# A two-layer block in float32r: the order of the first projection's column chunks

## The chip, the cores and the metric

The kernel runs on one core of a Trainium2 chip. The metric is the device time of one execution in microseconds (us). Engines: PE is TensorE (matrix products and transposes), ACT is ScalarE, DVE is VectorE, POOL is GpSimd, SP is SyncE, which here only issues transfers.

## What is computed

The reference has two layers on 256 tokens of 1024 channels. The change lies in the first layer's attention, whose first step is one wide projection `z = u @ w_in`, u being the normed input:

```
u = rms_norm(h, g_mix[i])
z = u @ w_in[i]
q_a, k_a, v_a, q_b, k_b, v_b, f_b, gate_logits = jnp.split(z, SPLIT_POINTS, axis=-1)
# widths:  512  128  128  512  512  512  8  2048
y_a = sliding_window_attention(q_a (8 heads), k_a, v_a (2 heads), sinks) @ w_br_swa[i]
# forgetting attention, per head:
log_f = log_sigmoid(f_b + b_forget);  c = cumsum(log_f)
s = q_b k_b^T * scale + c[query] - c[key], causal;  softmax;  times v_b
y_b = (that) @ w_br_fox[i]
mixed = gates[0] * y_a + gates[1] * y_b;  h = h + mixed @ w_mix_out[i]
```

A feed-forward part, an embedding gate, and a second layer follow. They are not touched.

## The kernel before, in words

**Products.** A float32 product is made of three passes. Both operands are split into an upper half (rounded to float32r) and a lower half (the rest), and PE computes upper x upper, upper x lower and lower x upper into the same PSUM bank (`mm3`, L1587 to L1589). So every piece of weight goes through a small pipeline: SP loads it into one of 8 slots of `raw`; ACT copies it into `w_hi` (one of 4 slots, L552); DVE subtracts and writes `w_lo` (L982); PE uses both. Counting semaphores tie the steps: `landed`, `hi_done`, `lo_done`, `units_used`. A piece is called a unit: two contraction tiles of 128 rows by up to 512 columns. Each unit takes 12 products (2 contraction tiles x 2 row tiles x 3). ACT and DVE run `AHEAD` = 3 units ahead of PE.

**Order.** Each engine has its own program, written out by hand, in order. `CH1` lists the column chunks of `w_in`, four units each. Before: chunk 0 has k_a, v_a and the 8 forget columns (264 columns), then q_a, q_b, k_b, v_b (512 each), then four chunks of gate logits, which PE works on in turn with the heads of the attention. Chunks use PSUM banks 0, 1 and 2, 3 alternately.

**Start.** SP issues the first half of x (two transfers), unit 0, the second half of x, then units 1 to 7, small vectors and the constant tables. ACT issues g_mix, the identity, and the forget columns of all four units of chunk 0 as one transfer (L617). PE runs 14 filler products of ones (`ones_products`), transposes g_mix and the first half of x (L1667), and runs 5 more fillers. ACT and DVE copy the transposed x, scaled, as upper and lower half (`wide_hi` L572, `wide_lo` L998), in turn with the splits of units 0 to 2.

**Eviction of the chunks.** ACT copies each chunk out of its banks, scaled by the norm's factor (`to_nat`, L612): queries and keys to `nat`, from where PE transposes them one chunk later (`natT_bank`) and DVE copies them to `qaT`, `ka_pad`, `qbT`, `kb_pad` (L1031, L1041, L1019); values go to `va_pad` and `vb_pad`; the forget columns go to `fz`.

**Forget gates.** DVE adds the bias; ACT computes ln(1 + exp(-|f|)) by Abs, Exp, Ln (L668, L670, L672); DVE forms the logs; PE sums them over the tokens by products with a triangle of ones (L1738 to L1740, `cum_done`); ACT and DVE copy the sums as upper and lower half (L675, L1127). `pick_tables` (L1094, L1096) makes on DVE a table of 0 and 1 for each of the 8 forgetting heads, with two casts each; a product of that table with the sums adds them to a head's scores. Before, all this runs inside chunks 1 to 4.

**Heads.** The loop over n = 0 to 19 has 16 heads, 8 of the sliding window, then 8 forgetting ones. In iteration n each engine does:

- PE: the 12 products of unit 20 + n, the scores of head n (L1773), the transposition of the probabilities of head n - 2 (`head_pt`, L1675), the output of head n - 3 (`head_pv`, L1686, L1687)
- ACT: the upper half of unit 23 + n, the copy of the transposed probabilities of head n - 2 (L605), the exponentials of head n (L595), which need DVE's row minima
- DVE: the lower half of unit 23 + n, scores and row minima of head n (L1051, `head_min`), the probabilities of head n - 1 (L1061, `head_norm`)

## Time and profile before

| | |
|---|---|
| median of 3 runs | 857.9 us (857.74 to 858.56) |
| profiled execution, its own time | 857.91 us |
| its span in the profile | 856.2 us |
| PE busy | 837.1 us, 98% of the span |
| DVE busy | 609.5 us, 71% |
| ACT busy | 464.6 us, 54% |
| POOL busy | 52.3 us, 6% |
| transfers | 170.45 MB, mean 199 GB/s |

The span runs from the first to the last instruction of the profiled execution; its own time contains a little more around it. Busy time of PE counts a product from its start to its modelled end, and products overlap, so the distance between two starts tells more than the duration of one. "Idle before" a group of instructions is given with what released the engine from its wait.

### The profile page before, as it was taken

To read this page: it belongs to the slowest core of one execution; us is meant where nothing else is said; L and a number is where in the kernel's file an instruction comes from. 1 tells how busy PE (TensorE), PEld (TensorE's weight loads), DVE (VectorE), ACT (ScalarE), POOL (GpSimd) and SP (SyncE) were. 2 spreads that over 40 slices of the span, in tenths; PEclk is the share of its full clock that TensorE was granted. 3 is DMA by queue.
4 is the path that set the end of the run, shared out by engine and by line. 5 is a ranking of instruction groups with operands and counts; after the bars stand their busy time and mean duration, and the time that the engine had idled before them with its cause. 6 is when DMAs were issued, how large, how long until landed. Compare 5 with 4: busy or idle time off the path is not lost.

```text
span 856.2 us, 12217 instructions
## 1 busy us (share of the span) xinstructions
PE 837.1 (98%) x4240; PEld 707.7 (83%) x4240; DVE 609.5 (71%) x947; ACT 464.6 (54%) x739; POOL 52.3 (6%) x68
## 2 busy tenths in 40 slices
PE   7999999999999999999999999999998999999996
PEld 7888888889888888877888888888887888888885
DVE  3666665867888888898767986565676766556656
ACT  4745665446555555677744446445444454445443
POOL 3000000102000000110200000011000000000000
PEclk9999999999999999999999999999999999999999
DMA  9764443597999999633664664545544465664641
GB/s 303 262 168 139 123 124 124 157 370 257 360 331 337 335 325 353 215 113 110 222 181 140 172 208 125 162 147 170 182 128 146 146 200 181 210 195 148 204 139 49
DMA packets 87560, 170.45 MB, mean 199 GB/s; under 512 B 7088, under 2 KB 33944, under 8 KB 87520
## 3 DMA queue, kind: packets, MB, share of 16 engines
q1 hardware_dynamic: 81040, 142.53, 51.9%
q0 software_dynamic: 5280, 27.30, 9.2%
q8 instruction: 23, 0.38, 0.2%
q10 hardware_dynamic: 1200, 0.10, 0.1%
q14 instruction: 17, 0.14, 0.0%
HBM read 168.84 MB, written 1.05 MB: 198 GB/s over the span
## 4 chain that ended last, share of the span: by engine, by line
PE 92%; DVE 3%; issue 1%; ACT 1%; DMA 1%; POOL 0%; ACTq 0%; DVEq 0%; POOLq 0%
PE B L1587 20%; PE B L1589 19%; PE B L1588 19%; PE B L1625 15%; PE B L1627 8%; PE B L1667 2%; PE B L1773 1%; PE B L1686 1%; PE B L1675 1%; DMA raw<-in_w_in_dram 1%; DVE w_lo L982 1%; PE B L1687 1%; PE B L1942 1%; PE B L1953 1%; DVE Z L1324 0%
## 5 line engine op out<-in xcount | busy, mean ns | idle before, releaser
L982 DVE TENSOR_TENSOR w_lo<-raw,w_hi 128x1024 fp32r<-128x1024 f32 (+3 forms) x156 | 187.1, 1210 | 80.8 <-ACT w_hi L552 79.0
L1587 PE MATMUL B<-w_hi,xT 128*128 128x512 f32 (+3 forms) x584 | 231.2, 396 | 3.8 <-DVE w_lo L982 3.1
L1589 PE MATMUL B<-w_hi,xT 128*128 128x512 f32 (+3 forms) x584 | 224.3, 384 | 0.0
L1588 PE MATMUL B<-w_lo,xT 128*128 128x512 f32 (+3 forms) x584 | 223.8, 383 | 0.0
L552 ACT ACTIVATE w_hi<-raw 128x1024 fp32r<-128x1024 f32 (+3 forms) x156 | 158.8, 1030 | 85.4 <-PE B L1589 80.6
L1587 PEld LDWEIGHTS B<-w_hi,xT 128*128 128x128 f32 x584 | 110.8, 190 | 24.5 <-issue 3.2
L1589 PEld LDWEIGHTS B<-w_hi,xT 128*128 128x128 f32 x584 | 110.5, 189 | 21.7
L1588 PEld LDWEIGHTS B<-w_lo,xT 128*128 128x128 f32 x584 | 110.9, 190 | 19.4
L1625 PE MATMUL B<-xT,w_hi 128*128 128x512 f32 x352 | 124.6, 398 | 1.8 <-DVE xT L1327 1.6
L1627 PE MATMUL B<-xT,w_lo 128*128 128x256 f32 x352 | 98.8, 281 | 0.0
L1552 DVE TENSOR_TENSOR w_lo<-raw,w_hi 128x1024 fp32r<-128x1024 f32 x60 | 71.7, 1221 | 29.0 <-ACT w_hi L949 29.0
L949 ACT ACTIVATE w_hi<-raw 128x1024 fp32r<-128x1024 f32 x60 | 62.0, 1054 | 41.2 <-PE B L1627 32.0
L1220 DVE TENSOR_TENSOR w_lo<-raw,w_hi 128x1024 fp32r<-128x1024 f32 x56 | 66.9, 1220 | 21.1 <-ACT w_hi L755 20.2
L1625 PEld LDWEIGHTS B<-xT,w_hi 128*128 128x128 f32 x352 | 66.1, 188 | 18.3 <-DVE xT L1327 1.8
L1587 PE MATMUL B<-w_hi,sT 128*128 128x512 f32 x200 | 79.3, 396 | 0.3 <-DVE w_lo L982 0.2
L1625 PE MATMUL B<-sT,w_hi 128*128 128x512 f32 x224 | 79.2, 397 | 0.0
L1589 PE MATMUL B<-w_hi,sT 128*128 128x512 f32 x200 | 78.1, 391 | 0.0
L1588 PE MATMUL B<-w_lo,sT 128*128 128x512 f32 x200 | 77.9, 390 | 0.0
L755 ACT ACTIVATE w_hi<-raw 128x1024 fp32r<-128x1024 f32 x56 | 57.6, 1053 | 35.2 <-PE B L1627 32.0
L1627 PEld LDWEIGHTS B<-xT,w_lo 128*128 128x128 f32 x352 | 66.5, 189 | 0.4
L1627 PE MATMUL B<-sT,w_lo 128*128 128x256 f32 x224 | 62.9, 281 | 0.0
L1228 DVE SCALAR_TENSOR_TENSOR Z<-Z,small 128x1536 f32<-128x1536 f32 x28 | 50.7, 1811 | 1.4 <-DMA Z<-in_w_ada_dram 1.4
(231 smaller groups left out, 993.3 us busy)
## 6 DMA issues: line engine op xcount, KB each, us to landing
raw<-in_w_in_dram SPq DMA_DIRECT2D x84, 512.0 KB, 3.7
raw<-in_w_ff_dram SPq DMA_DIRECT2D x64, 512.0 KB, 7.5
Z<-in_w_ada_dram POOLq DMA_DIRECT2D x32, 768.0 KB, 7.7
raw<-in_w_ffn_gate_dram SPq DMA_DIRECT2D x44, 256.0 KB, 3.6
raw<-in_w_ffn_up_dram SPq DMA_DIRECT2D x44, 256.0 KB, 4.4
raw<-in_w_ffn_down_dram SPq DMA_DIRECT2D x20, 512.0 KB, 4.4
raw<-in_w_mix_out_dram SPq DMA_DIRECT2D x8, 512.0 KB, 3.7
raw<-in_w_ple_gate_dram SPq DMA_DIRECT2D x8, 512.0 KB, 4.5
```

The costliest lines, as they stand in the source:

```text
L552: nc.scalar.activation(w_hi[:, u % SPLIT, :, 0:n], raw[:, st.slot[u], :, 0:n], ACT.Copy).then_inc(hi_done, 1)
L755: nc.scalar.activation(w_hi[:, u % SPLIT, :, :], raw[:, st.slot[u], :, :], ACT.Copy).then_inc(hi_done, 1)
L949: nc.scalar.activation(w_hi[:, u % SPLIT, :, :], raw[:, st.slot[u], :, :], ACT.Copy).then_inc(hi_done, 1)
L982: nc.vector.tensor_tensor(w_lo[:, u % SPLIT, :, 0:n], raw[:, st.slot[u], :, 0:n], w_hi[:, u % SPLIT, :, 0:n].bitcast(F32), ALU.subtract).t ...
L1220: nc.vector.tensor_tensor(w_lo[:, u % SPLIT, :, :], raw[:, st.slot[u], :, :], w_hi[:, u % SPLIT, :, :].bitcast(F32), ALU.subtract).then_in ...
L1228: nc.vector.scalar_tensor_tensor(ada_acc[:, 1536 * q:1536 * (q + 1)], ada_raw[:, q, :], silu_now, ada_acc[:, 1536 * q:1536 * (q + 1)], ALU ...
L1552: nc.vector.tensor_tensor(w_lo[:, u % SPLIT, :, :], raw[:, st.slot[u], :, :], w_hi[:, u % SPLIT, :, :].bitcast(F32), ALU.subtract).then_in ...
L1587: nc.tensor.matmul(bank, xh, wh, start=start, stop=False)
L1588: nc.tensor.matmul(bank, xh, wl, start=False, stop=False)
L1589: return nc.tensor.matmul(bank, xl, wh, start=False, stop=stop)
L1625: nc.tensor.matmul(B[:, i, :], w_hi[:, s, kk, cols], x2[:, kt0 + kk, :, :].rearrange("p e n -> p (e n)"), start=first and kk == 0, stop=False)
L1627: m = nc.tensor.matmul(B[:, i, SEQ:2 * SEQ], w_lo[:, s, kk, cols], x2[:, kt0 + kk, 0, :], start=False, stop=last and kk == 1)
```

## The change

1. The chunks are regrouped: q_a; k_a, v_a and half of v_b; q_b; k_b; the other half of v_b and the forget columns (264 columns); then the gates as before. A unit of the second chunk is loaded in two parts.
2. The forget columns are part of their chunk's load, and ACT's separate transfer is gone.
3. Unit 0 is loaded as two transfers of one contraction tile each (`first_in`, then `landed[0]`), and split and used in two pieces (`first_hi`, `first_lo`). ACT splits the first piece ahead of the first copy of x. PE runs 7 fillers instead of 5.
4. The forget gates come in the fifth chunk now, so their bias, Abs, Exp and Ln are done before head 0, their sums by PE behind the scores of n = 1, the copies of the sums in n = 1 (ACT) and n = 2 (DVE), and the tables in n = 3 to 6, two heads each.

```diff
-    CH1 = [(264, [(0, 512, 256)]), (512, [(0, 0, 512)]), (512, [(0, 768, 512)]),
-           (512, [(0, 1280, 512)]), (512, [(0, 1792, 512)])] + [(512, [(0, 2312 + 512 * i, 512)]) for i in range(4)]
-    for _, parts in CH1:
+    CH1 = [[(0, 0, 512)], [(0, 512, 256), (256, 1792, 256)], [(0, 768, 512)], [(0, 1280, 512)], [(0, 2048, 264)]]\
+        + [[(0, 2312 + 512 * i, 512)] for i in range(4)]
+    for parts in CH1:
...
                 if half == 0:
-                    load(0)
+                    for kk, name in enumerate((sem("first_in"), landed[0])):
+                        sp.dma_start(raw[:, 0, kk, :], w_in1[kk * P:(kk + 1) * P, 0:512]).then_inc(name, 16)
             for u in range(1, RAW):
                 load(u)
...
-            act.dma_start(raw[:, 0:4, :, 256:264].rearrange("p s k n -> p (s k) n"),
-                          w_in1.rearrange("(k p) n -> p k n", p=P)[:, :, 2304:2312]).then_inc(sem("forget_cols_in"), 16)
             act.wait_ge(sem("vec_T"), 1)
             nc.scalar.activation(vec[:, 0:8], B[:, 7, 0:8], ACT.Copy).then_inc(sem("vec_done"), 1)
             act.wait_ge(sem("vec_done"), 1)
+            act.wait_ge(sem("first_in"), 16)
+            nc.scalar.activation(w_hi[:, 0, 0, :], raw[:, 0, 0, :], ACT.Copy).then_inc(sem("first_hi"), 1)
             wide_hi((2,), xT_hi, 0, V_GMIX)
-            act.wait_ge(sem("forget_cols_in"), 16)
-            split_to(0)
+            act.wait_ge(landed[0], 16)
+            nc.scalar.activation(w_hi[:, 0, 1, :], raw[:, 0, 1, :], ACT.Copy).then_inc(hi_done, 1)
+            done[0] = 1
...
+            for c in range(5):
                 split_to(4 * c + 3 + AHEAD)
...
+                    if c == 1:
+                        for dup in range(2):
+                            to_nat(1, t, bank[:, 0:P].rearrange("p (g d) -> p g d", g=2), r,
+                                   nat[:, 1, t, 0:2 * P].rearrange("p (g u d) -> p g u d", g=2, u=2)[:, :, dup, :])
+                        to_nat(1, t, bank[:, P:2 * P].rearrange("p (h d) -> p h d", d=HD), r, values(va_pad)[:, t, :, :])
+                        last = to_nat(1, t, bank[:, 2 * P:4 * P].rearrange("p (h d) -> p h d", d=HD), r, values(vb_pad)[:, t, 0:4, :])
+                    elif c == 4:
+                        to_nat(0, t, bank[:, 2 * P:2 * P + 8], r, fz[:, t, :])
+                        last = to_nat(0, t, bank[:, 0:2 * P].rearrange("p (h d) -> p h d", d=HD), r, values(vb_pad)[:, t, 4:8, :])
...
                     last.then_inc(sem("evac"), 1)
+                if n == 0:
+                    act.wait_ge(sem("f_logit"), 1)
+                    nc.scalar.activation(fa, fz, ACT.Abs).then_inc(sem("f_act"), 1)
+                    act.wait_ge(sem("f_act"), 1)
+                    nc.scalar.activation(fa, fa, ACT.Exp, scale=-1.0).then_inc(sem("f_act"), 1)
+                    act.wait_ge(sem("f_act"), 2)
+                    nc.scalar.activation(fa, fa, ACT.Ln, bias=1.0).then_inc(sem("f_act"), 1)
+                if n == 1:
+                    act.wait_ge(sem("cum_done"), 1)
+                    nc.scalar.activation(cum[:, :], B[0:LO_ROW + HEADS, 7, 0:KEYS], ACT.Copy).then_inc(sem("cum_hi"), 1)
                 if 0 <= n - 2 < 16:
                     head_pt(n - 2)
                 if n < 16:
...
-            wide_lo((2,), xT_hi, xT_lo, 0, V_GMIX)
-            split_to(0)
+            for kk, (upper_half, lower_half) in enumerate(((sem("first_hi"), sem("first_lo")), (hi_done, lo_done))):
+                if kk:
+                    wide_lo((2,), xT_hi, xT_lo, 0, V_GMIX)
+                dve.wait_ge(upper_half, 1)
+                nc.vector.tensor_tensor(w_lo[:, 0, kk, :], raw[:, 0, kk, :], w_hi[:, 0, kk, :].bitcast(F32),
+                                        ALU.subtract).then_inc(lower_half, 1)
+            done[0] = 1
             wide_lo((3,), xT_hi, xT_lo, 2, V_GMIX)
             split_to(1)
...
+            dve.wait_ge(sem("consts_in"), 16)
+            for k in range(4):
                 split_to(4 * k + 7 + AHEAD)
-                pick_tables(range(2 * k - 2, 2 * k if k < 3 else HEADS))
...
+            dve.wait_ge(sem("forget_in"), 16)
+            dve.wait_ge(sem("evac"), 5)
+            for t in range(TILES):
+                last = nc.vector.tensor_tensor(fz[:, t, :], fz[:, t, :], bf, ALU.add)
+            last.then_inc(sem("f_logit"), 1)
+
+            for n in range(2 * HEADS + 4):
+                split_to(20 + n + AHEAD)
+                if n == 0:
+                    dve.wait_ge(sem("f_act"), 3)
+                    dve.wait_ge(sem("lf_zero"), 1)
+                    for row in (0, LO_ROW):
+                        nc.vector.scalar_tensor_tensor(lf[:, :, row:row + HEADS], fz, 0.0, fa, ALU.min, ALU.subtract).then_inc(sem("log_f"), 1)
+                if n == 2:
                     dve.wait_ge(sem("cum_hi"), 1)
                     low = slice(LO_ROW, LO_ROW + HEADS)
                     nc.vector.tensor_tensor(cum[low, :], B[low, 7, 0:KEYS], cum[low, :].bitcast(F32), ALU.subtract).then_inc(sem("cum_lo"), 1)
...
+                if 3 <= n < 7:
+                    pick_tables((2 * n - 6, 2 * n - 5))
                 if n < HEADS:
                     head_min(n, distance, 2.0 ** -(n + 1), nsink[:, n:n + 1])
...
-            ones_products(5)
+            ones_products(7)
...
+                    if u:
+                        pe.wait_ge(lo_done, u + 1)
+                        unit_pair(u, xT_hi, xT_lo, 2 * kp, banks, kp == 0, kp == 3)
+                    else:
+                        for kk, lower_half in enumerate((sem("first_lo"), lo_done)):
+                            pe.wait_ge(lower_half, 1)
+                            for t in range(TILES):
+                                rows = slice(t * P, (t + 1) * P)
+                                m = mm3(B[:, banks[t], :], xT_hi[:, kk, rows], xT_lo[:, kk, rows], w_hi[:, 0, kk, :], w_lo[:, 0, kk, :],
+                                        kk == 0, False)
+                        m.then_inc(units_used, 1)
                         pe.wait_ge(sem("x_in1"), 32)
                         transposes((4, 5), lambda t, k: h[:, t, (4 + k) * P:(5 + k) * P], "wt_done")
...
-                if c == 2:
-
-                    pe.wait_ge(sem("log_f"), 2)
-                    pe.wait_ge(sem("consts_in"), 16)
-                    pe.wait_ge(sem("ones"), 1)
...
-                        pe.wait_ge(sem("tables"), 3)
                         pe.wait_ge(sem("natT_copied"), 4)
+                    if n == HEADS:
+                        pe.wait_ge(sem("tables"), 4)
                         pe.wait_ge(sem("cum_lo"), 1)
...
+                if n == 1:
+
+                    pe.wait_ge(sem("log_f"), 2)
+                    pe.wait_ge(sem("consts_in"), 16)
+                    pe.wait_ge(sem("ones"), 1)
+                    for c0 in (0, P):
+                        nc.tensor.matmul(B[0:LO_ROW + HEADS, 7, c0:c0 + P], lf[:, 0, :], upper, start=True, stop=True)
+                    nc.tensor.matmul(B[0:LO_ROW + HEADS, 7, SEQ:KEYS], lf[:, 0, :], ones, start=True, stop=False)
+                    nc.tensor.matmul(B[0:LO_ROW + HEADS, 7, SEQ:KEYS], lf[:, 1, :], upper, start=False, stop=True).then_inc(sem("cum_done"), 1)
                 if 0 <= n - 3 < 16:
                     k = n - 3
+                    if k == 0:
+                        pe.wait_ge(sem("cum_lo"), 1)
```

How the rows stand on the engines is shown at three places. The first is DVE from the lower half of unit 22 to the minima of head 0; in brackets is what a row waits for. Before:

```order
L1094 CAST pick<-cst 64x128
L1096 CAST pick<-cst 8x128
L1041 COPY Z<-B 64x2x256 [waits natT_bank,pads_zero]
L1041 COPY Z<-B 64x2x256
L1041 COPY Z<-B 64x2x256 [waits natT_bank]
L1041 COPY Z<-B 64x2x256
L982 TENSOR_TENSOR w_lo<-raw,w_hi 128x1024 [waits hi_done]
L1051 ISA Z,small<-B,cst,small 128x128 [waits scores_done]
```

With the change:

```order
L1040 COPY Z<-B 64x2x256 [waits natT_bank]
L1040 COPY Z<-B 64x2x256
L1121 TENSOR_TENSOR small<-small 128x8 [waits evac,forget_in]
L1121 TENSOR_TENSOR small<-small 128x8
L981 TENSOR_TENSOR w_lo<-raw,w_hi 128x1024 [waits hi_done]
L1130 SCALAR_TENSOR_TENSOR small<-small 128x2x8 [waits lf_zero,f_act]
L1130 SCALAR_TENSOR_TENSOR small<-small 128x2x8
L1050 ISA Z,small<-B,cst,small 128x128 [waits scores_done]
```

The casts are gone from ahead of the copies; the bias and the logs of the forget gates stand between the copies and the minima of head 0.

The second is ACT at the same place, from the eviction of the fifth chunk to head 0. Before:

```order
L612 ACTIVATE Z<-B,small 128x8x64 [waits pads_zero,units_used]
L612 ACTIVATE Z<-B,small 128x8x64 [waits pads_zero]
L552 ACTIVATE w_hi<-raw 128x1024 [waits units_used,landed7]
L595 ACT_TABLE_LOAD
L595 ACTIVATE Z,small<-Z,small 128x128 [waits rmin_done]
```

With the change:

```order
L613 ACTIVATE Z<-B,small 128x4x64
L553 ACTIVATE w_hi<-raw 128x1024 [waits units_used,landed7]
L679 ACTIVATE small<-small 128x16 [waits f_logit]
L681 ACTIVATE small<-small 128x16 [waits f_act]
L683 ACT_TABLE_LOAD
L683 ACTIVATE small<-small 128x16 [waits f_act]
L596 ACT_TABLE_LOAD
L596 ACTIVATE Z,small<-Z,small 128x128 [waits rmin_done]
```

The three functions of the forget gates and a load of the tables moved in ahead of head 0's exponentials, which keep their own load.

The third is DVE in iteration n = 3 of the heads' loop, with the change; before, no cast stands in the loop:

```order
L981 TENSOR_TENSOR w_lo<-raw,w_hi 128x1024 [waits hi_done]
L1098 CAST pick<-cst 64x128
L1100 CAST pick<-cst 8x128
L1098 CAST pick<-cst 64x128
L1100 CAST pick<-cst 8x128
L1050 ISA Z,small<-B,cst,small 128x128 [waits pt_done,scores_done]
```

Four casts stand between the lower half and the minima, in n = 3, 4, 5 and 6.

## Rows read from the trace of the kernel before

**Rows 1.** The page, the chain that ended last, shares of the span by engine.

```profile
PE 92%; DVE 3%; issue 1%; ACT 1%; DMA 1%; POOL 0%; ACTq 0%; DVEq 0%; POOLq 0%
```

**Rows 2.** Chain of waits up to PE's first weight product: start us, us, what.

```profile
1.92 7.83 DMA raw<-in_w_in_dram
...
9.78 0.65 ACT w_hi L552
...
10.45 0.72 DVE w_lo L982
...
11.31 0.56 PE B L1587
```

**Rows 3.** Timeline of the start: start us, us, engine line op out<-in xcount.

```profile
5.30 1.97 PE L1667 MATMUL B<-cst,h 128*128 128x128 f32 x8
...
6.52 0.84 ACT L572 ACTIVATE xT<-B,vec 128x256 fp32r<-128x256 f32 x2 [0.94 <-PE B L1667]
...
6.92 1.31 PE L1694 MATMUL B<-ones_r 128*128 128x128 f32 x5
...
7.48 0.88 DVE L998 SCALAR_TENSOR_TENSOR xT<-B,vec,xT 128x256 fp32r<-128x256 f32 x2 [5.89 <-ACT xT L572]
```

**Rows 4.** Timeline of PE in the first chunk, 264 columns each.

```profile
17.11 0.41 PE L1587 MATMUL B<-w_hi,xT 128*128 128x264 f32 x1
...
17.33 0.31 PE L1588 MATMUL B<-w_lo,xT 128*128 128x264 f32 x1
...
17.48 0.28 PE L1589 MATMUL B<-w_hi,xT 128*128 128x264 f32 x1
...
17.60 0.28 PE L1587 MATMUL B<-w_hi,xT 128*128 128x264 f32 x1
```

**Rows 5.** DMA issues near 1.8 us: KB each, us from issue to landing.

```profile
h<-in_x_dram SPq DMA_DIRECT2D x1, 256.0 KB, 3.5
raw<-in_w_in_dram SPq DMA_DIRECT2D x1, 256.0 KB, 6.3
```

**Rows 6.** Chain of waits around the forget gates' sums, and the product behind them.

```profile
44.28 0.44 PE B L1738 x4
...
45.15 0.23 PE B L1587
```

**Rows 7.** Timeline of ACT's forget chain and DVE's lower half of the sums.

```profile
33.27 0.22 ACT L668 ACTIVATE small<-small 128x16 f32<-128x16 f32 x1
...
33.75 1.28 ACT L672 ACT_TABLE_LOAD   x1
...
35.05 0.21 ACT L672 ACTIVATE small<-small 128x16 f32<-128x16 f32 x1
...
57.92 0.56 DVE L1127 TENSOR_TENSOR cum<-B,cum 8x384 fp32r<-8x384 f32 x1
```

**Rows 8.** Timeline at the end of the fifth chunk and the first head.

```profile
67.47 0.21 DVE L1094 CAST pick<-cst 64x128 fp32r<-64x128 f32 x1
...
67.70 1.03 PE L1667 MATMUL B<-cst,nat 128*128 128x128 f32 x8
...
69.33 2.80 DVE L1041 COPY Z<-B 64x512 f32<-64x512 f32 x4
...
72.23 0.89 PE L1773 MATMUL B<-Z 128*128 128x128 f32 x4 [0.77 <-issue]
...
74.22 0.40 ACT L595 ACTIVATE Z<-Z,small 128x128 f32<-128x128 f32 x1 [2.81 <-DVE small L1051]
```

**Rows 9.** Timeline in the heads' loop: ACT and DVE in turn, then head 5.

```profile
88.64 1.23 DVE L982 TENSOR_TENSOR w_lo<-raw,w_hi 128x1024 fp32r<-128x1024 f32 x1 [1.33 <-ACT w_hi L552]
...
90.57 0.40 ACT L595 ACTIVATE Z<-Z,small 128x128 f32<-128x128 f32 x1 [1.59 <-DVE small L1051]
...
99.29 0.55 DVE L1061 TENSOR_SCALAR Z<-Z,small 128x128 f32<-128x128 f32 x2
...
101.13 0.49 PE L1675 MATMUL B<-cst,Z 128*128 128x128 f32 x3
```

67 lines of the change are left out of this document (12 added, 55 removed).

## Prediction

> **What bounds the kernel now.** I read the chain of waits first. TensorE (PE) holds 92% of it [rows 1], so time is won only by starting PE's stream sooner, by running it at the higher clock sooner, or by closing a gap in it, and anything that makes PE wait is paid in full. So the question is where PE idles near the edit. Four places count.
>
> Before the first weight product the chain is a transfer: a load of raw that ACT issues at 1.92 and that lands 7.83 us later; PE's first product starts at 11.31 [rows 2]. That load is the forget columns, 8 KB a unit in pieces of 32 bytes; the first split waits for it. PE's own operand is ready long before: the transposes of x run from 5.30, their copies on ACT and DVE end at 8.36 (7.48 + 0.88), and the five filler products end near 8.2, so PE idles for about 3 us [rows 3].
>
> The second place is the clock. The granted-clock column reads full from the start, so I go by the distance between starts. Products of 264 columns start 0.22 us apart until 17.33 (17.11 to 17.33), which is 1.2 GHz, and 0.12 apart afterwards (17.48 to 17.60), which is 2.4 GHz. Products of 512 columns take 0.23 each at the high level, as the chain's step at 45.15 shows [rows 4, 6]. The rise comes 6.02 us after PE resumed at 11.31.
>
> The third place is the end of the fifth chunk. Call T the start of the last transposes of queries and keys, 67.70. PE stops for 0.77 us until 72.23: its first scores wait for DVE's copies, 69.33 to 72.13 [rows 8].
>
> The fourth is the heads' loop. There ACT and DVE hand work to each other: upper halves (ACT), lower halves (DVE), row minima (DVE), exponentials (ACT), next upper halves. DVE waits 1.33 us for ACT's half at 88.64, ACT waits 1.59 us for DVE's minima at 90.57 [rows 9]. Both look idle, but this ring has no slack of its own: whatever is put between two of its links delays all later heads. Only PE's lead against the ring is slack.
>
> **The change part by part.** Durations come from the profiled execution, 857.91 us with a span of 856.2; it stands 0.01 above the median 857.9.
>
> *Start.* The forget load goes. The first contraction tile of the first unit, 256 KB, is now a transfer of its own, issued where the first unit's load was, at 1.81. It shows nowhere before, so I bound it. The half of x beside it, same shape, takes 3.5 us from issue to landing, and the first unit's 256 KB, in rows half as long and beside the 32-byte pieces, takes 6.3 [rows 5]. That is 5.3 or 8.1 on the clock of the trace. I take 5.3, because shape and row length are x's and the small pieces are gone. ACT then splits the tile (at most the 0.65 us of a piece of 528 columns [rows 2]) and is free before it can copy x at 6.52. DVE ends x's lower halves at 8.36 as before, and PE needs 0.15 more, as from 11.17 to 11.31 [rows 2, 3]. Seven fillers instead of five, about 0.22 us each from 6.92, end near 8.5, so they just fill the wait. PE starts at 8.6: **-2.7**. The second tile's lower half is ready about 0.7 us later, while six slow products last 2.6, so it costs nothing. Its point of decision: a landing after 5.9 moves everything by as much.
>
> *Clock.* Eight transposes (1.7 us) and 19 products ran at the low level before; that cost 19 x 0.10 and 0.9, or 2.8 us. Now PE has no idle time from the transposes at 5.3 on [rows 3], if the fillers close the gap. With the same 6.0 us of uninterrupted work the rise comes at 11.3, and the 2.7 us from 8.6 on run at half rate: 1.35 lost. The bounds are nothing lost (a rise at 8.6) and 3.0 (6.0 us counted from 8.6). I take the middle, since 6.0 us is the only delay that a row shows: **-1.45**. That wide products and not narrow ones fill the low stretch changes nothing: the work done in each us of it is half either way.
>
> *Order of the chunks.* 48 products of 264 columns and 4 x 48 of 512 stand in either program, and as many transposes, so the reordering costs PE nothing. One new wait: unit 2 needs its lower half, and DVE's comes after the transposes behind unit 0, x's upper halves (0.84), the split (1.04), and its own 1.23. PE reaches unit 2 in 3.2 us after those transposes' first bank, and the sum with latencies is 3.5: **+0.3**. Later units have a margin of over 1 us. The four more transfers of the second chunk's two parts and the 1 MB more in the first eight units lie on SP and the DMA engines, whose units PE takes 10 us and more after they are issued. Chunk 2's eviction has eight small copies instead of two, on ACT while PE has banks to spare. If that cover went, it would be worth their extra 1.3 us.
>
> *Sums of the forget gates.* The eight products leave the third chunk, 44.28 to 45.15 [rows 6]: **-0.87**. They come back behind the scores of n = 1, and count in the next term.
>
> *Heads.* I follow the ring relative to T. Fifth-chunk units are narrow now (1.44 us each), so three wide splits for units 20 to 22 crowd before T. ACT may split unit 22 only once unit 18 is used, at T - 1.2, and DVE's lower half ends at T + 1.15. The eight casts that sat in front of the copies are gone (67.47 to 69.33), so the copies start then and end at T + 3.95. PE's first scores start at T + 4.05 and not T + 4.53 [rows 8]. Then the forget chain, which now runs here and not in the second chunk: DVE's adds to T + 4.2; ACT's Abs, Exp, table load and Ln, 2.0 us (33.27 to 35.26) [rows 7], to T + 6.26; and then the table has to go back to Exp, 1.28 more, T + 7.54. Head 0's exponentials began at 74.22, T + 6.52 [rows 8]. The ring is late by 1.02. At n = 2 DVE's lower half of the sums comes into it, 0.56 [rows 7]. At n = 3 to 6 four casts each stand between split and minima: 8 took 1.86, so 0.93 each, 3.72 in all [rows 8]. Sum of lateness at n = 6: 1.02 + 0.56 + 3.72 = 5.30. PE's transposition of head 5's probabilities starts at 101.13 and these were ready at 99.84 (99.29 + 0.55) [rows 9], a slack of 1.29; with 0.1 for the signal PE is late by 5.30 + 0.1 - 1.29: **+4.1** against T. That takes in the returned sums and the 0.48 saved on the first scores, since they only move PE within waits that the ring now sets. After n = 6 nothing is added and PE, whose period is the longer, is not held again.
>
> A rule of the skill speaks against this part. [rows 7] show a table load of 1.28 us with Ln starting 0.02 behind it. The Trainium skill, ScalarE: Activation LUTs, section What ACT_TABLE_LOAD costs, says that a switch costs the load of about 1283 ns and a drain of about 1380 more. The trace agrees on the load and shows no drain.
>
> **Sum:** -2.7 - 1.45 + 0.3 - 0.87 + 4.1 = -0.6, and 857.9 - 0.6 = **857.3 us**. The gain at the start is real, and nearly all of it goes back in the heads.
>
> **The rivals.**
> 1. *The casts and sums are hidden.* DVE is idle 1.33 us an iteration, which speaks for it; that they stand behind the split and ahead of the minima speaks against it. Then PE is later only by the sums, 0.87 - 0.48 = 0.4: 4.3 us faster, 853.6. Chance 0.10.
> 2. *The clock rises as PE reaches the weights*, at 8.6, after 3.3 us of transposes and fillers: 1.35 less, 855.9. The same transposes and five fillers brought no rise by 8.2 before, which speaks against. Chance 0.13.
> 3. *The clock counts from the first weight product* (the fillers or the transposes don't serve): it rises at 14.6, costs 3.0, 1.65 more: 858.9. Chance 0.13.
> 4. *Slower: the first piece lands late.* Its 256 KB queue behind x's 512 KB on the same engines. At 8.1, as the first unit did, ACT stands in front of it with the copies of x queued behind, and PE starts at 8.1 + 0.65 + 0.84 + 1.0 + 0.15 = 10.75. That is 2.15 more, and with PE idle for 2.3 us again the clock counts from there, 1.65 more: 861.1. It decides from 5.9 on, and turns the sign at about 6.5. Chance 0.09.
> 5. *A table switch costs a drain as well.* Two switches lie in the ring now, and if the time until the next work were twice the load's 1.28, each would add 1.28: 859.9. Rows 7 refute it for Ln; only the load that goes back could differ. The page named above would make it 1.38 each. Chance 0.02.
>
> **Numbers.** 0.50 for the forecast, whose own range is 856.1 to 858.5 (the three tenths of unit 2, half a microsecond for the landing, half for the clock), and 0.03 for what I don't see. About 0.2% or 1.7 us is what a measurement of this kernel tells from no change: the bounds are 856.2 and 859.6. Faster: all of rival 1, most of rival 2, a fifth of the forecast: 0.31. Slower: rivals 4 and 5 and a little of rival 3: 0.12. Same: 0.57. The range leaves out rivals 1 and 4: 855.0 to 859.6.
>
> **What would show it.** Start: PE's first 512-column product at 8.6 with almost no idle time before it, ACT's wait for the first piece under 0.3 us. Clock: starts 0.43 apart up to about 11, then 0.23. Heads: two table loads on ACT around T + 5 and T + 6.3, PE waiting for DVE's probabilities in iterations 3 to 6, in all about 3 us, and casts between split and minima. Wrong if PE shows no wait there (rival 1), if the first product starts after 9.5 (rival 4), or if the distance of 0.43 lasts beyond 13 (rival 3).

## The result: slower, and the profile after

| | before | changed |
|---|---|---|
| median, runs side by side | 857.82 us (4 runs) | 862.54 us (4 runs: 858.78, 863.09, 862.29, 862.79) |
| ratio | | 1.0045, 95% interval 1.0031 to 1.0059 |
| profiled execution | 857.91, span 856.2 | 858.78, span 857.1 |
| share of PE in the chain | 92% | 85% |

The forecast was 857.3, with a range of 855.0 to 859.6. The changed kernel is 0.45% slower and lies above the range. Its profiled execution is the fastest of the four, 3.8 us under their median, so this one trace does not show what the kernel usually does. A second profile of the same kernel does (the first experiment).

The page of the changed kernel, shares of the chain that ended last by engine, against [rows 1]:

```profile
PE 85%; DVE 6%; ACT 4%; issue 3%; DMA 1%; POOL 0%; ACTq 0%; DVEq 0%; POOLq 0%
```

DVE and ACT now hold a tenth of the chain. Where PE waits is in the changed kernel's waits of PE up to 110 us (engine, line, what it waited for: us in total, times, longest):

```profile
PE B L1681 <- DVE Z L1060: 2.1, 4, 0.8
PE B L1700 <- DVE ones_r L1073: 1.6, 1, 1.6
PE B L1706 <- DMA cst<-in_tables_dram: 1.2, 1, 1.2
PE B L1692 <- DVE sT L1065: 1.2, 2, 0.6
```

L1681 is the transposition of probabilities, as forecast. L1692 (`head_pv`) waits until DVE has read the output of the pair of heads before out of bank 7, as its lower half; no step of the forecast had this. L1706 waits for the identity before PE can transpose anything.

**The start.** PE's timeline of the changed kernel (start us, us, engine, line, operation), against [rows 3, 4]:

```profile
6.14 0.27 PE L1706 MATMUL B<-cst,vrows 8*128 8x8 f32 x1 [1.25 <-DMA cst<-in_tables_dram]
6.34 1.97 PE L1673 MATMUL B<-cst,h 128*128 128x128 f32 x8
7.96 1.74 PE L1700 MATMUL B<-ones_r 128*128 128x128 f32 x7
9.50 0.73 PE L1593 MATMUL B<-w_hi,xT 128*128 128x512 f32 x1
10.03 0.63 PE L1594 MATMUL B<-w_lo,xT 128*128 128x512 f32 x1
10.46 0.51 PE L1595 MATMUL B<-w_hi,xT 128*128 128x512 f32 x1
10.81 0.39 PE L1593 MATMUL B<-w_hi,xT 128*128 128x512 f32 x1
11.03 0.39 PE L1594 MATMUL B<-w_lo,xT 128*128 128x512 f32 x1
```

The first product starts at 9.50, not at 8.6. The identity came 1 us later than before, and ACT's wait for the first piece ended at 6.87, not 5.3:

```profile
6.87 0.63 ACT L622 ACTIVATE w_hi<-raw 128x512 fp32r<-128x512 f32 x1 [0.24 <-DMA raw<-in_w_in_dram]
```

The distance between products falls from 0.43 to 0.23 at about 10.7 (here 1.2 GHz gives way to 2.4), a little before the forecast's 11.3.

**The heads.** T, the start of the last transposes of queries and keys, is 63.04, against 67.70. Timeline of the changed kernel around head 0's logs and in the heads' loop, ACT, DVE and PE, against [rows 8, 9]:

```profile
63.04 1.04 PE L1673 MATMUL B<-cst,nat 128*128 128x128 f32 x8
...
67.66 1.28 ACT L683 ACT_TABLE_LOAD   x1
68.95 0.22 ACT L683 ACTIVATE small<-small 128x16 f32<-128x16 f32 x1
69.18 1.28 ACT L596 ACT_TABLE_LOAD   x1
...
70.48 0.40 ACT L596 ACTIVATE Z<-Z,small 128x128 f32<-128x128 f32 x1
...
80.24 0.55 PE L1681 MATMUL B<-cst,Z 128*128 128x128 f32 x3 [0.82 <-DVE Z L1060]
...
100.64 0.55 PE L1681 MATMUL B<-cst,Z 128*128 128x128 f32 x3 [0.43 <-DVE Z L1060]
...
101.23 0.42 DVE L1065 TENSOR_TENSOR sT<-B,sT 128x256 fp32r<-128x256 f32 x1 [0.64 <-ACT sT L610]
101.80 0.67 PE L1692 MATMUL B<-Z 128*128 128x256 f32 x2 [0.61 <-DVE sT L1065]
```

The exponentials of head 0 start at T + 7.44 (forecast 7.54). PE's transposition for head 5 starts at T + 37.60; before it was T + 33.43 [rows 9], so +4.17 against a forecast of +4.1. But right behind it PE stops once more, for 0.61 us, and starts `head_pv` at 101.80. That wait is not in the sum.

### The profile page after: what moved, and what is told of

It is laid out like the page before. It is cut to its first block, busy times and chain, and to the rows that moved or that the text cites. A ratio compares the mean times of both kernels' runs of the same rounds, so it can differ in the third digit from the quotient of the medians.

```text
span 857.1 us, 12239 instructions
## 1 busy us (share of the span) xinstructions
PE 837.2 (98%) x4242; PEld 705.3 (82%) x4242; DVE 609.9 (71%) x948; ACT 465.7 (54%) x742; POOL 52.2 (6%) x68
## 4 chain that ended last, share of the span: by engine, by line
PE 85%; DVE 6%; ACT 4%; issue 3%; DMA 1%; POOL 0%; ACTq 0%; DVEq 0%; POOLq 0%
PE B L1593 18%; PE B L1595 18%; PE B L1594 18%; PE B L1631 14%; PE B L1633 7%; PE B L1673 2%; DVE w_lo L981 1%; ACT w_hi L553 1%; PE B L1692 1%; DMA Z<-in_w_ada_dram 1%; PE B L1681 1%; PE B L1779 1%; PE B L1970 1%; PE B L1959 1%; ACT Z L596 1%
## 5 line engine op out<-in xcount | busy, mean ns | idle before, releaser
L1633 PEld LDWEIGHTS B<-xT,w_lo 128*128 128x128 f32 x352 | 66.5, 189 | 0.4
```

The source lines that it names most:

```text
L1633: m = nc.tensor.matmul(B[:, i, SEQ:2 * SEQ], w_lo[:, s, kk, cols], x2[:, kt0 + kk, 0, :], start=False, stop=last and kk == 1)
```

## Experiments

All times are medians of runs beside the kernel before. The median of before moves by some tenths from one set of runs to the next (857.66 to 858.43), so experiments of different sets are compared by their ratios to before, with the 95% interval in brackets. Where the text says that a piece of weight lands at some time, that is the start of ACT's split of it.

**1. The changed kernel again, unedited.** 

> The changed kernel unchanged, to see what its usual execution looks like: its profiled one took 858.8 us, the three others 862.3 to 863.1. Theory A (clock): the 4 us are the clock. The profile shows products of 512 columns 0.43 us apart far beyond 10.8, to 17 or later, and the heads' part as in the first profile. Theory B (transfers): the identity or the first piece lands 2 us or more later than in the first profile and PE's first weight product starts after 11.5. Theory C (heads): the start is the same, and PE waits 4 us more in the heads.

Measured 861.46 (859.8 to 862.33, 6 runs), ratio 1.0032 [1.0017, 1.0047]; profiled execution 862.0. Its timelines of ACT and PE:

```profile
9.10 0.63 ACT L622 ACTIVATE w_hi<-raw 128x512 fp32r<-128x512 f32 x1 [3.22 <-DMA raw<-in_w_in_dram]
```

```profile
7.21 1.74 PE L1700 MATMUL B<-ones_r 128*128 128x128 f32 x7
11.42 0.79 PE L1593 MATMUL B<-w_hi,xT 128*128 128x512 f32 x1 [2.47 <-DVE xT L997]
...
14.14 0.63 PE L1593 MATMUL B<-w_hi,xT 128*128 128x512 f32 x1
14.57 0.45 PE L1594 MATMUL B<-w_lo,xT 128*128 128x512 f32 x1
14.86 0.39 PE L1595 MATMUL B<-w_hi,xT 128*128 128x512 f32 x1
```

This is rival 4 in place and direction, and of the three theories theory B comes nearest: the piece lands at 9.10, PE idles 2.47 us and starts at 11.42, no sooner than before, and the clock rises some 3 us behind that. T is 66.02 instead of 63.04, and the profiled times differ by 3.2: the two executions are nearly the same but for their first 15 us. Theory C falls, since the heads' part repeats. The mean GB/s in the stretch from 4 to 6 us was 214 in the first profile and 183 here.

**2. Six more narrow fillers** (14 to 20). 

> 20 filler products instead of 14 ahead of the first transposes, which fill the 1.2 us in which PE waited for the identity (4.9 to 6.1). Theory A (an interruption of PE's work before the first weight product sets when the clock rises): the slow executions go, all at 858 to 859. Theory B or C: the times stay at 858.8 and 862.7, or 0.1 to 0.3 longer where a filler delays the transposes.

```diff
-            ones_products(14)
+            ones_products(20)
```

Measured 861.69 (10 runs), ratio 1.0037 [1.0026, 1.0048]: nothing gained. In its trace the piece lands at 8.29, the first product starts at 10.61 and the distance falls only at about 16.2. The added products keep PE at work ahead of the transposes, from 1.64 to 9.84 (8.10 + 1.74) without a gap, and the weight products behind them are 0.43 apart all the same. So theory A falls.

**3. The casts out of the heads' loop**, to DVE's fourth-chunk loop, behind its copies. 

> The tables' 16 casts go back from the heads' loop to DVE's idle time behind the copies of the first two chunks; nothing else changes. My account of the heads says that the four times 0.93 us in the ring cost PE about 3 us in waits for the probabilities and for the pairs' outputs: 2.8 to 3.5 us faster than the changed kernel in the same clock state (855.5 or 859.5). Rival (the casts are hidden by DVE's idle time, the waits come from the late start of head 0): under 0.5 us faster.

```diff
-                if 3 <= n < 7:
-                    pick_tables((2 * n - 6, 2 * n - 5))
...
+                if k < 2:
+                    for i in (4 * k, 4 * k + 2):
+                        pick_tables((i, i + 1))
```

Measured 857.97 (10 runs), before 858.43, ratio 0.9992 [0.9982, 1.0001]. That is about 3.5 us under the changed kernel of experiment 1, run in the same set, against the 3.72 that the sum gave the casts. The rival (hidden casts, under 0.5 us) falls. One wait of PE is left in the heads, 0.82 us at 81.88.

**4. The kernel before with 14 more narrow fillers** in front of its first product. 

> The kernel before with 19 filler products instead of 5 behind the first transposes, which bridge the 3 us of idle time to its first weight product at 11.3 and nothing else. Theory A (uninterrupted work brings the clock up): the clock rises at or before 11.5 and not at 17.3, 2 to 2.8 us faster, 855.1 to 855.9. Rival (fillers and transposes don't count): the rise stays at 17.3, no change within 0.3.

```diff
-            ones_products(5)
+            ones_products(19)
```

Measured 858.27 (10 runs), ratio 1.0003 [0.9993, 1.0012]: no change, though the idle time in front of the first product fell to 0.26 us. The first products are 0.22 apart as before, and the distance falls only while PE does the transposes at 14.35. Theory A falls here too.

**5 to 8. Four edits on top of experiment 3** (before: 857.66). Each of the first three comes out about 1 us under experiment 3 by the ratio (0.9983, 0.998 and 0.998 after 0.9992). Their intervals overlap that of experiment 3, so for each gain alone the traces say more than the medians.

**5.** Weights first: SP issues the first piece ahead of x's first half. 

> The run picks with one more edit: SP issues the first weight piece ahead of the first half of x, not behind it. Theory 1 (the piece is late because it queues behind 512 KB of x): it lands at 5.5 to 6, no longer gates ACT; x lands about 0.7 us later, PE's first weight product starts near 9.5 in every execution, against 9.5 to 11.4 over four profiles: 0.7 to 1.5 us faster than picks (858.0 in the median). Theory 2 (the first transfers are slow whatever their order, since the engines move under 200 GB/s from 4 to 6 us): the start stays between 10 and 11.4, and the time within 0.3.

```diff
+                if half == 0:
+                    sp.dma_start(raw[:, 0, 0, :], w_in1[0:P, 0:512]).then_inc(sem("first_in"), 16)
                 for t in range(TILES):
...
                 if half == 0:
-                    for kk, name in enumerate((sem("first_in"), landed[0])):
-                        sp.dma_start(raw[:, 0, kk, :], w_in1[kk * P:(kk + 1) * P, 0:512]).then_inc(name, 16)
+                    sp.dma_start(raw[:, 0, 1, :], w_in1[P:2 * P, 0:512]).then_inc(landed[0], 16)
```

856.59 (11 runs), ratio 0.9983 [0.9974, 0.9992]. ACT no longer waits (5.69), but PE now waits 0.7 us for x; the first product starts at 9.33 in the trace, against 10.31 in that of experiment 3.

**6.** Bias between the copies: DVE adds the forget bias behind the copies of the first of the two banks. 

> The run picks with one more edit: DVE adds the forget gates' bias between the copies of the two banks of the last transposes, and not behind all four copies, so ACT's Abs, Exp, table load, Ln and table load start 1.2 us earlier. My account (head 0's exponentials are late by 1.0 us through that chain, and PE waits 0.8 us once for the probabilities): the 0.8 us wait goes, 0.6 to 0.9 us faster than picks. Rival (the wait comes from the sums' copy in iteration 2 alone): the wait stays over 0.5, under 0.2 us faster.

```diff
-                    copy_T_halves(3, kb_pad, (4, 5), 2, 3)
+                    copy_T_halves(3, kb_pad, (4, 5), 2, 3, add_bias)
...
+                    if i == 0 and between is not None:
+                        between()
```

856.36 (11 runs), ratio 0.998 [0.997, 0.9989]. The 0.82 us wait is gone; 0.38 at the first scores took its place. Head 8's scores start at T + 37.92 instead of T + 38.98.

**7.** POOL's broadcasts late: its two broadcasts (sinks, forget bias; 128 rows of 32 bytes each) are issued behind its memsets. 

> The run picks with one more edit: POOL issues the two broadcasts of 8 numbers to 128 partitions (sinks, bias of the forget gates) behind its memsets at 7.8 us and not at 1.4 and 2.1. Theory 3 (their 256 tiny pieces hold up the engines between 4 and 6 us, when 160 to 214 GB/s are moved): over 280 GB/s from 4 to 6, the first piece lands by 6.8, 0.7 to 1.5 us faster than picks. Rival (they cost nothing): the same rates, within 0.3 us of picks.

```diff
-            pool.dma_start(sink, swa_sinks.partition_broadcast(P).rearrange("p a n -> p (a n)")).then_inc(sem("sinks_in"), 16)
-            pool.dma_start(bf, b_forget.partition_broadcast(P).rearrange("p a n -> p (a n)")).then_inc(sem("forget_in"), 16)
...
+            pool.wait_ge(sem("pads_zero"), 4)
+            pool.dma_start(sink, swa_sinks.partition_broadcast(P).rearrange("p a n -> p (a n)")).then_inc(sem("sinks_in"), 16)
+            pool.dma_start(bf, b_forget.partition_broadcast(P).rearrange("p a n -> p (a n)")).then_inc(sem("forget_in"), 16)
```

856.02 (855.7 to 856.96, 10 runs), ratio 0.998 [0.9971, 0.999]. The spread is 1.3 us, where experiment 3 had 2.9. In its trace the piece lands at 6.94, and 272 GB/s are moved from 4 to 6 us, a little short of the 6.8 and the 280 that theory 3 asked for, against 7.99 and 161 in experiment 3.

**8.** One piece: unit 0 loaded, split and used whole, as before the change. 

> The run picks with the first unit loaded, split and used in one piece, so only the changed order of the chunks is left of the start. If the two pieces are worth what the trace suggests (PE starts on the first half while DVE makes the second; ACT splits ahead of x's copy), PE's first product starts 0.7 to 1.3 us later: 0.7 to 1.3 us slower than picks. Rival (the landing sets the start, and ACT's waiting for the first piece with x's copies queued behind it costs as much as the split gains): within 0.3, or faster.

```diff
-                    for kk, name in enumerate((sem("first_in"), landed[0])):
-                        sp.dma_start(raw[:, 0, kk, :], w_in1[kk * P:(kk + 1) * P, 0:512]).then_inc(name, 16)
+                    load(0)
```

859.48 (11 runs), ratio 1.0019 [1.001, 1.0028]; the unit lands at 9.61, the first product starts at 12.07. So the split in two does earn something, about 2.3 us against experiment 3 by the ratios, more than the 0.7 to 1.3 expected.

**9. The first three of them together** on experiment 3 (weights first, bias between, broadcasts late). 

> All edits that gained, together: casts out of the heads' loop, bias added between the copies, first weight piece ahead of x, POOL's broadcasts late. The first weight product can't start before 9.2, where x's lower halves end, so the two edits on the transfers don't add up: about 1.0 for the start and 1.0 for head 0 below picks, near 855.3 with the kernel before at 857.7, a ratio of 0.9970 to 0.9978. If all four added up it would be 0.9965 or lower.

854.85 (5 runs, before 858.2), ratio 0.996 [0.9947, 0.9974]. The ratio is below the 0.9970 to 0.9978 expected, and its interval also holds what full addition would give. The traces bear out the reason given: T is 64.67 in experiment 3, 63.97 and 63.98 with either edit on the transfers and 63.60 with both, so those two don't add up in full.

**10. The same with wide fillers**, 8 and 5 of 512 columns over a slot of `w_lo` that DVE sets to 1 first. 

> all_four with filler products of 512 columns, 8 and 5 of them, in place of 14 and 7 of 128 columns. Theory W (narrow fillers bring the clock up less surely than wide ones, since in five profiles they ran for up to 8 us without a rise): the clock rises before or shortly after the first weight product at 9.3 and not at 12 to 15, 1.0 to 1.8 us faster than all_four. Rival (only time since the last idle stretch counts): the rise stays near 12.8, within 0.3.

```diff
-                    nc.tensor.matmul(B[:, 6, 0:P], ones_r[:, :], ones_r[:, :], start=True, stop=True)
+                    nc.tensor.matmul(B[:, 6, :], ones_r[:, :], w_lo[:, 3, 0, :], start=True, stop=True)
```

853.02 (5 runs), ratio 0.9939 [0.9926, 0.9953]. Timeline of PE:

```profile
2.18 3.78 PE L1708 MATMUL B<-w_lo,ones_r 128*128 128x512 f32 x8 [2.18 <-DVE ones_r L1078]
5.89 0.27 PE L1714 MATMUL B<-cst,vrows 8*128 8x8 f32 x1
6.22 1.23 PE L1681 MATMUL B<-cst,h 128*128 128x128 f32 x8
7.21 1.42 PE L1708 MATMUL B<-w_lo,ones_r 128*128 128x512 f32 x5
8.85 0.50 PE L1601 MATMUL B<-w_hi,xT 128*128 128x512 f32 x1 [0.23 <-DVE xT L999]
9.19 0.40 PE L1602 MATMUL B<-w_lo,xT 128*128 128x512 f32 x1
9.43 0.39 PE L1603 MATMUL B<-w_hi,xT 128*128 128x512 f32 x1
```

The eight transposes take 1.23 us instead of 1.97, and the weight products stand 0.23 apart from the second on: the high level is there when the transposes run. By the medians this is 1.8 us faster than experiment 9, the upper end of theory W.

**11. The kernel before with the broadcasts late.** 

> The kernel before with only POOL's two broadcasts issued behind its memsets. If they are what holds up the first transfers, the forget columns land earlier than at 9.7, PE's first weight product starts before 10.8, and it is 0.5 to 1.5 us faster than the kernel before. Rival (the 1,024 pieces of 32 bytes set that landing whatever else is in flight): start at 11.3, within 0.3.

856.71 (11 runs), ratio 0.9979 [0.997, 0.9988]. The landing moves from 9.78 to 8.15, and the first product from 11.31 to 9.68. So this part of what the changed kernel needed is useful without it too.

**12. The changed kernel with only the bias between the copies.** 

> The changed kernel, casts still in the heads' loop, with only the bias added between the copies. My account says that lateness in the ring of ACT and DVE adds up link by link: the 1.0 us taken out in front of head 0 comes off the sum although the waits appear in iterations 3 to 7: 0.8 to 1.1 us faster than the changed kernel (ratio to before 1.0022 to 1.0026 after 1.0035). Rival (the casts set the waits alone): within 0.3.

859.75 (7 runs), ratio 1.0017 [1.0002, 1.0033]. The interval holds both the 0.8 to 1.1 us of my account and no gain at all against experiment 1 (1.0032), so the median decides nothing. The trace does: the scores of head 8 start at T + 41.34, against T + 42.43, which is 1.09 earlier.

**13. The changed kernel with only the wide fillers.** 

> The changed kernel with 512-column filler products (8 and 5 instead of 14 and 7 of 128) and nothing else. Theory A (the term of the clock costs the changed kernel 1.3 to 2.7 us in its usual execution, and wide fillers end that): the gate opens before the first weight product at about 10, the products stand 0.23 apart from the start, and the time is about 2 us under the changed kernel's usual 861.5 to 862.5, that is 859.5 to 860.5, spread as before because the landing is untouched. Theory B (the clock follows the end of PE's last idle stretch, whatever ran before it): while the first piece lands at 8 to 9, PE idles after the fillers, the rise comes 3 us and more behind the first product as in the repeat of the changed kernel, and the time stays at 861 to 862.5.

860.28 (858.25 to 862.29, 6 runs, before 858.05), ratio 1.0033 [1.0021, 1.0046]. The profiled execution bears out theory A (the weight products 0.23 apart from the second on, T = 61.87, the earliest of the changed kernel's), and the median lies in its range; but as a ratio it is that of experiment 1 (1.0032). The trace shows one execution in which the piece was there early; what the clock does in those where it is late was not seen, so for these theory B is not refuted.

**14. The kernel before with wide fillers**, 8 and 12. 

> The kernel before with 512-column fillers, 8 and 12 instead of 14 and 5 of 128, which close its idle stretch in front of the first weight product at 11.3. Theory A: the clock is at its high level at 11.3, the 19 slow products of 264 columns and eight slow transposes become fast, 19 x 0.10 + 0.9 = 2.8 us, so 855.0 to 855.6, where 19 narrow fillers in that place gave nothing (1.0003). Theory B (what the narrow fillers did not do, wide ones do not either): 857.7 to 858.3. If A holds, part of what the changed kernel was to gain was to be had without it.

856.21 (11 runs), ratio 0.9981 [0.9972, 0.999]. The products stand 0.12 apart from 11.26 on; 0.66 us of the 2.8 expected come back as a wait for unit 2, whose lower half is no earlier than before:

```profile
5.81 1.09 PE L1668 MATMUL B<-cst,h 128*128 128x128 f32 x8
...
11.06 0.36 PE L1588 MATMUL B<-w_hi,xT 128*128 128x264 f32 x1 [1.38 <-DVE w_lo L982]
11.26 0.28 PE L1589 MATMUL B<-w_lo,xT 128*128 128x264 f32 x1
11.38 0.28 PE L1590 MATMUL B<-w_hi,xT 128*128 128x264 f32 x1
...
15.73 0.36 PE L1588 MATMUL B<-w_hi,xT 128*128 128x264 f32 x1 [0.66 <-DVE w_lo L982]
```

Theory A holds for the clock, where 14 more narrow products had given nothing (experiment 4); the high level even outlasts 1.38 us without work. The time is 0.6 us above theory A's range, about the wait.

**15. The changed kernel with only the broadcasts late.** 

> The changed kernel with POOL's two broadcasts (sinks and bias) issued behind its memsets and nothing else. Theory A (the first piece lands late because the broadcasts' small packets share the engines with it): the first piece lands at about 7 in nearly every execution, the spread of the times shrinks from some 4 us to 1.5, and the median falls by 2 to 3 us, to 858.5 to 860. Theory B (x's 512 KB ahead of it alone make it late): no change, 861 to 862.5, with the same spread.

859.3 (858.39 to 860.01, 11 runs), ratio 1.0015 [1.0006, 1.0024]. Theory A holds: the piece lands at 6.59 in the trace, the time is in the range given, and the spread is 1.6 us, against 2.5 to 4.7 in the five sets of runs that have the changed kernel's heads and the early broadcasts. By the ratios the gain is 1.5 us against experiment 1 and 2.6 against the first result; the intervals of this one and of experiment 1 overlap. The stretch from 4 to 6 us in windows of the two traces (its length; busy time of PE, PEld, DVE, ACT, POOL with counts; then clock, DMA share, GB/s), first of this one, then of experiment 1:

```profile
4.00:6.00 2.00, 1.42 (x8) 1.21 (x8) 0.00 (x0) 0.18 (x1) 2.00 (x2) 1.00 0.98 296
```

```profile
4.00:6.00 2.00, 1.50 (x8) 1.29 (x8) 0.00 (x0) 0.18 (x1) 2.00 (x3) 1.00 0.82 183
```

Without the broadcasts the DMA engines moved 296 GB/s there, and 183 with them.

**16, 17. Both start fixes in the kernel before, beside the version of experiment 10.** 

> The kernel before with 512-column fillers (8 and 9) and POOL's two broadcasts issued late: the same start fixes as the best version so far, without the regrouped chunks. Theory A (the two are separate costs, a landing and a clock): the first weight product starts at about 9.7 as with the late broadcasts alone and all products run 0.12 apart, so the last transposes of queries and keys start at 67.7 - 1.5 - 2.1 = 64.1 and the time is 854.3 to 854.8; the regrouped chunks with all their fixes (853.0) are then worth only 1.3 to 1.8 us. Theory B (one buys what the other buys): 856.0 to 856.5, as either alone, and the regrouping is worth over 3 us.

> The best version again, beside the one above on the same chip: 852.7 to 853.4, whatever theory holds; it is here so that the two can be compared directly.

Before with both: 854.9 (12 runs, before 857.91), ratio 0.997 [0.9961, 0.998]. The version of experiment 10: 853.45 (7 runs), ratio 0.9959 [0.9944, 0.9974]. Theory A is much the nearer: alone the fixes gave 1.5 and 1.8 us by the medians, together they give 3.0. With the same fixes at the start, the regrouping with its own three repairs (casts early, bias between, weights first) is worth 1.4 us by the medians; by the two ratios it is 0.9, their intervals overlap, and the same program had 0.9939 in experiment 10. In the two traces T is 2.3 us earlier (62.13 against 64.44) and head 8 stands 0.6 us later after it.

## Why the forecast was wrong, step by step

One table carries the argument. T is the start of the last transposes of queries and keys; "head 8" is the start of head 8's scores on PE, less T; "rest" is the profiled execution's time less T.

| profiled execution | first product | T | head 8 | time | rest |
|---|---|---|---|---|---|
| before | 11.31 | 67.70 | 37.35 | 857.91 | 790.2 |
| before, wide fillers | 11.06 | 65.56 | 37.35 | 855.88 | 790.3 |
| before, broadcasts late | 9.68 | 65.88 | 37.34 | 856.15 | 790.3 |
| changed | 9.50 | 63.04 | 42.43 | 858.78 | 795.7 |
| changed, again | 11.42 | 66.02 | 42.42 | 862.00 | 796.0 |
| changed, wide fillers | 8.69 | 61.87 | 42.44 | 858.25 | 796.4 |
| changed, broadcasts late | 8.91 | 63.72 | 42.42 | 859.63 | 795.9 |
| changed, bias between | 9.65 | 64.43 | 41.34 | 858.70 | 794.3 |
| casts early | 10.31 | 64.67 | 38.98 | 856.77 | 792.1 |
| casts early, bias between | 10.71 | 65.76 | 37.92 | 856.71 | 791.0 |
| best (experiment 10) | 8.85 | 61.92 | 37.92 | 853.08 | 791.2 |

The time is a sum of two parts that hardly touch each other: what happens before T, which varies from execution to execution, and what comes after, which for one kernel repeats to 0.02 us at head 8 and to 0.7 us in "rest". The forecast erred in both.

**Start: the step that failed.** "I take 5.3, because shape and row length are x's and the small pieces are gone." Where the changed kernel's order of loads was untouched, ACT's split of the piece began at 6.36 (experiment 13), 6.87, 7.33 (experiment 12), 7.99 (experiment 3), 8.29 (experiment 2), 8.39 (experiment 6) and 9.10 (experiment 1); 5.3, the bound I took, was reached in none, and three lie above the upper bound, 8.1. The mechanism was right: by "a landing after 5.9 moves everything by as much", landings at 6.87 and 9.10 put the first product at 9.57 and 11.8, and it started at 9.50 and 11.42. Wrong was the size of the landing. By the rest of 796.0, the median of 862.54 means T = 66.5 in the usual execution, an estimate from the table. That is 1.2 us earlier than before, where the sum had 4.7 (2.7, 1.45 and 0.87, less 0.3). No execution at that median was profiled; the nearest one is experiment 1's, 862.00 with T at 66.02. Rival 4 described this rightly in kind (the place, the idle time of 2.3 against 2.47 us, the later clock) and had a chance of 0.09. That its 861.1 us comes near is in part luck: it had the start 0.7 us too early and the heads' term 1.7 too small, and the clock's loss, 3.0, too large by 1.5. The reason for 5.3 was a false analogy: x's transfers are issued first, and the piece stands behind their 512 KB; issued ahead of x, it no longer held up ACT (5.69 in experiment 5's trace). "The small pieces are gone" was half true: those of the forget columns were, but POOL's two broadcasts of 32-byte rows were still there. Issuing these later brought the spread from 2.5 us and more down to 1.6, with a landing at 6.59 (experiment 15). One execution with the broadcasts early had 6.36, so what they do is make a late landing usual.

**Clock.** The forecast had the rise at 11.3 and took 1.35 of the 2.8 us as lost. In the first profile it came 1.2 us behind the first product and cost 0.5; in the repeat it came 3 us behind and cost 1.5 (eight starts in 3.44 us instead of 1.95). So the size was within its bounds. The reasoning was wrong, though. "With the same 6.0 us of uninterrupted work the rise comes" does not survive experiment 2, where PE worked on narrow fillers and transposes for 8.2 us without a gap, and the rise came another 6.4 us after that, 0.8 of them idle. Experiments 4 and 14 differ in the fillers' width and gave 1.0003 and 0.9981: which work PE did counted, and not its length alone. The forecast's remark that wide and narrow products make no difference in the low stretch is about the weight products; no run tests it.

**Unit 2 and the sums.** In the first profile the parts before T are -1.8 for the start, -2.3 for the clock, +0.2 for unit 2 (starts 0.42 apart at 16.28 and 16.70 instead of 0.23) and -0.87 for the sums: -4.8, where T moved by -4.66. These two small terms stand.

**Heads: right, but one hand-off short.** The lateness of the ring was 5.30 by the sum; the exponentials of head 7 start at 99.76 - 63.04 = T + 36.72 and not 99.01 - 67.70 = T + 31.31, which is 5.41. The casts were priced at 3.72, and taking them away gave 3.45 at head 8. But PE waits for more than one hand-off of the ring. I took the slack of one, the probabilities, 1.29 [rows 9]. The other comes in every second iteration: `head_pv` begins a pair of heads only when DVE has read the pair before out of bank 7 (`pe.wait_ge(sem("aT_lo"), m_)`). Before, that read ended at 100.91 (100.49 + 0.42) and PE began at 101.46, a slack of 0.55. The rows of the kernel before, with head 8's scores behind them:

```profile
100.49 0.42 DVE L1066 TENSOR_TENSOR sT<-B,sT 128x256 fp32r<-128x256 f32 x1 [0.65 <-ACT sT L609]
...
101.46 0.60 PE L1686 MATMUL B<-Z 128*128 128x256 f32 x2
...
105.05 0.82 PE L1773 MATMUL B<-Z 128*128 128x128 f32 x4
```

and head 8's scores in the changed kernel:

```profile
105.47 0.82 PE L1779 MATMUL B<-Z 128*128 128x128 f32 x4
```

By the forecast's own method the slack of 0.55 gives 5.30 + 0.1 - 0.55 = 4.85; PE was late there by (101.80 - 63.04) - (101.46 - 67.70) = 5.00, and by 5.08 at head 8. The step that failed is the slack of 1.29, taken as the only one: the term was +4.1 and measured 5.1 at head 8. By the rest it is 5.5 to 6.1, and 5.8 with the average of 796.0 against 790.2. Most of what lies behind head 8 arises in one place, about 153 us after T: there the first profile loses 0.3 us more, the repeat 0.4 and experiment 13 0.7, of which 0.5 is shown as a wait of PE for the lower half of a piece of weight. Why that piece is late there was not followed.

PE's waits cost more than their idle time. The six waits of the first profile (four at L1681, two at L1692) add up to 3.3 us, but from the scores of head 2 to those of head 8 the distance grew by 4.8 us (42.43 - 11.71 against 37.35 - 11.43); with one wait of 0.82 left (experiment 3) its interval grew by 1.04. A product's modelled end lies some 0.16 us behind the start of its follower (0.39 against 0.23), so the profile's idle time starts about that much late. (The other 0.3 of the 5.1 is the sums' products, 0.9, less the 0.65 by which the first scores are earlier.)

**Rivals.** Rival 1 (casts hidden) is refuted by experiment 3, and by the rest of 796.0. Rival 5 (a drain at a table switch) did not occur: Ln starts 0.01 us behind its load, and the exponentials 0.02 behind the second one. The Trainium skill, ScalarE: Activation LUTs, section What ACT_TABLE_LOAD costs, adds about 1380 ns to a switch. The trace does not agree: the two loads here show 1.28 us each and no more. By rivals 2 and 3 the clock would have risen at the first weight product or 6.0 us behind it; in the changed kernel and its repeat it was 1.2 and 3.2 us behind it, so neither holds; with the narrow fillers of experiment 2 it was 5.6, near rival 3.

**In all.** Of the miss of 5.2 us (862.54 against 857.3), 3.5 lie before T (1.2 gained, by the estimate above, instead of 4.7) and 1.7 behind it (5.8 lost instead of 4.1).

## What to carry to other kernels

Where PE waits for several hand-offs of one ring of engines, find the one with the least slack before pricing what is put into the ring, and count a bank that has to be read out as one of them; the one nearest at hand need not be it. A transfer that stands behind others is priced from the last transfer that stood there, never from the first in the queue, and if its landing decides the sign, a second profile of the same kernel is worth more than a finer sum. Small work that looks free on an idle engine (four casts of 0.22 us an iteration, on a DVE that waits 1.33 us in it) costs nearly its full length when it stands between two links of the ring, 3.45 of 3.72 us here; behind the copies of the first two chunks it caused no wait of PE in the trace.

## What I had not expected of the hardware

- Two broadcasts in rows of 32 bytes slow the first transfers of a kernel. From 4 to 6 us the traces show 145 to 226 GB/s with them (257 in one of twelve) and 249 to 300 in the seven without; in the kernel before, the first landing came 1.6 us earlier without them. Whether it is their short rows or that POOL issues them was not separated.
- The shape of the fillers matters. With fillers of 128 columns the first weight products stood at the 1.2 GHz distance in all fourteen traces that have them; with fillers of 512 columns the transposes ahead of them took 1.09 to 1.23 us instead of 1.97, and the weight products stood at the 2.4 GHz distance from the second on, in each of the five traces that have them. It is worth 1.8 us in the kernel before (856.21 after 858.05, ratio 0.9981). The granted-clock column read 1.00 throughout the first 60 us; only the distance between starts shows the level.
- One kernel can have a spread of 4.3 us (858.78 to 863.09) with the same instructions. The two profiled executions of it are 3.2 us apart, 3.0 of that before T, where the landing of one 256 KB transfer and the clock behind it differ.
